# A hybrid encoder layer on one core: the first norm's scale moved behind the first eight tiles, and the final norm summed over five columns

## What is computed

```python
def rmsnorm(x, g):
    y = x * lax.rsqrt(jnp.mean(x * x, axis=-1, keepdims=True) + EPS)
    return y * g

h = rmsnorm(x, p['norm_mix'])
z = h @ w_in                       # 12 column groups; the first 1024 columns are q and k of the mLSTM
...                                # conv, mLSTM, forgetting attention, cross-attention, gates
mk, mv = split(rmsnorm(mem, g_mem) @ w_mem_kv, 2)
x = x + merged; x = x + peer(rmsnorm(x, p['norm_ffn']))
y = rmsnorm(x, norm_final)
```

## Time and profile before

| what | value |
|---|---|
| median of three runs | 2088.78 us |
| profiled execution | 2090.58 us |
| its span | 2088.9 us |
| TensorE busy | 2003.2 us (96%) |
| VectorE busy | 1430.3 us (68%) |
| ScalarE busy | 839.0 us (40%) |
| GpSimd busy | 818.8 us (39%) |
| chain of waits: TensorE / VectorE / DMA / ScalarE / GpSimd | 82 / 10 / 3 / 2 / 1% |
| first product of the first tile | 26.22 us |
| end of the last product of the experts' tiles | 2068.0 us |

### The profile page before, as it was taken

One profiled execution on the slowest core, in us unless ns is written; L12 is line 12 of the kernel. 1 busy time (PEld: TensorE's weight loads), 2 busy tenths in 40 slices (PEclk: granted clock), 3 DMA queues, 4 the chain that ended last, 5 costly groups with the idle time before them and its releaser, 6 DMA issues.

```text
span 2088.9 us, 34386 instructions
## 1 busy us (share of the span) xinstructions
PE 2003.2 (96%) x12642; PEld 1227.1 (59%) x12652; DVE 1430.3 (68%) x2691; ACT 839.0 (40%) x1244; POOL 818.8 (39%) x518
## 2 busy tenths in 40 slices
PE   5998998999999999999999999999999999999996
PEld 3745666667777787555555555555455555555553
DVE  5662555433336566989989989984787777777774
ACT  5334334344444433333345566563333333333331
POOL 5442111122234344465676667666343222222210
PEclk9999999999999999999999999999999999999998
DMA  5532112122334222456688999999999888888961
GB/s 200 138 128 94 41 41 85 68 80 72 137 126 146 102 72 75 148 202 232 213 330 314 353 360 358 354 351 397 382 369 372 332 328 329 329 332 334 346 232 46
DMA packets 180321, 467.12 MB, mean 224 GB/s; under 512 B 18600, under 2 KB 85168, under 8 KB 179448
## 3 DMA queue, kind: packets, MB, share of 16 engines
q1 hardware_dynamic: 102160, 248.28, 33.4%
q0 software_dynamic: 36864, 134.23, 17.5%
q10 hardware_dynamic: 41192, 83.22, 10.7%
HBM read 393.54 MB, written 72.14 MB: 223 GB/s over the span
## 4 chain that ended last, share of the span: by engine, by line
PE 82%; DVE 10%; DMA 3%; ACT 2%; POOL 1%; issue 1%; ACTq 0%; DVEq 0%
PE ps L1517 30%; PE ps L1904 27%; PE ps L1587 10%; PE ps L1533 3%; PE ps L1734 2%; DMA rows<-in_u_rows,rowi 1%; PE ps L1856 1%; PE ps L1857 1%; DVE rows L1363 1%; PE ps L1923 1%; PE ps L1699 1%; PE ps L1714 1%; POOL w_lo L485 1%; DVE hot L1425 1%; PE ps L1790 1%
## 5 line engine op out<-in xcount | busy, mean ns | idle before, releaser
L485 POOL TENSOR_TENSOR w_lo<-raw,w_hi 128x1024 bf16<-128x1024 f32 x229 | 508.5, 2223 | 760.9 <-ACT w_hi L570 759.8
L570 ACT ACTIVATE w_hi<-raw 128x1024 bf16<-128x1024 f32 x357 | 375.0, 1052 | 483.0 <-PE ps L1904 293.9
L1517 PE MATMUL ps<-act_hi,w_hi 128*128 128x448 bf16 (+1 forms) x1168 | 391.6, 346 | 9.8 <-DVE act_lo L973 8.6
L1517 PE MATMUL ps<-act_lo,w_hi 128*128 128x448 bf16 (+1 forms) x1168 | 391.4, 345 | 0.0
L1517 PE MATMUL ps<-act_hi,w_lo 128*128 128x448 bf16 (+1 forms) x1168 | 391.1, 345 | 0.0
L1904 PE MATMUL ps<-W_hi,w_hi 128*128 128x448 bf16 x992 | 350.3, 353 | 4.5 <-DVE W_lo L1465 4.5
L1904 PE MATMUL ps<-W_lo,w_hi 128*128 128x448 bf16 x992 | 350.3, 353 | 0.0
L1904 PE MATMUL ps<-W_hi,w_lo 128*128 128x448 bf16 x992 | 350.2, 353 | 0.0
L514 POOL DMA_INDIRECT rows<-in_v_units,rowi x128 | 151.4, 1183 | 412.2 <-DVE accS L1460 395.3
L1441 DVE TENSOR_TENSOR w_lo<-raw,w_hi 128x1024 bf16<-128x1024 f32 x128 | 156.7, 1224 | 115.4 <-ACT w_hi L570 110.5
L881 ACT ACTIVATE hb<-ps 128x448 f32<-128x448 f32 x128 | 69.6, 543 | 323.5 <-PE ps L1517 287.2
(11 more groups left out here) (355 smaller groups left out, 3197.3 us busy)
## 6 DMA issues: line engine op xcount, KB each, us to landing
raw<-in_u_units SPq DMA_DIRECT2D x128, 512.0 KB
raw<-in_v_units SPq DMA_DIRECT2D x128, 512.0 KB
raw<-in_units SPq DMA_DIRECT2D x101, 512.0 KB
hd<-hb ACTq DMA_DIRECT2D x128, 224.0 KB
gd<-gsb ACTq DMA_DIRECT2D x64, 448.0 KB
Gb<-gd SPq DMA_DIRECT2D x32, 896.0 KB
Hb<-hd SPq DMA_DIRECT2D x32, 896.0 KB
gz<-stage ACTq DMA_DIRECT2D x24, 288.0 KB, 2.1
```

What stands on the lines that cost most here:

```text
L485: pool.tensor_tensor(w_lo[:, k % RING, :], raw[:, k % RAW, :], w_hi[:, k % RING, :], ALU.subtract).then_inc(lo_ready, 1)
L570: act.activation(w_hi[:, k % RING, :], raw[:, k % RAW, :], ACT.Copy).then_inc(hi_ready, 1)
L1517: last = pe.matmul(ps[:, bank + half, 0:n], w[:, slot, col:col + P], x(k)[:, half * n:(half + 1) * n], start=(k == 0 and w is w_hi and x i ...
```

## The change

It has four parts.

1. **First eight tiles on x times the norm's weight.** ScalarE makes `raw_hi` = high half of x * par straight from x (an activation with the weight as scale), VectorE `raw_lo` by one operation. The eight tiles multiply with these, and `copy_tile` becomes a product: PSUM times `wk`, the row of 1/rms. The tiles turn over three pairs of banks (0 to 5), so tile k waits for the copy of tile k - 3. The squares, sums, root and rows of x are made while the tiles run: `x_sums`, `m_sums` and `x_rows` stand in tile 2, ahead of k = 1, 4 and 7. The rows of 1/rms are made in banks 6 and 7 and copied to `wk` by ScalarE. The normed activation itself (`mix_h`, `act_hi`, `act_lo`) is still made, between the copies; it is needed from the small tile on.
2. **VectorE makes the first four low halves.** GpSimd starts at unit 4, and only when VectorE has added both sets of squares.
3. **The memory's squares beside x's.** `mem_x` is issued by SyncE behind units 1 to 3, its squares follow unit 4 on ScalarE, its adds follow x's on VectorE. Unit 0 is issued by ScalarE between the two halves of x, `par` by SyncE ahead of everything; SyncE's first units wait for the second half of x, not the first. ScalarE loads the table of the square root at the very start.
4. **The final norm over five columns**, as in the norm before the experts. The adds of the squares no longer run one bank behind (`FIN_ADDS`); the eight products read 1/rms from PSUM.

The core of the diff:

```diff
@@ sync
-            sp.wait_ge(x_in[0], 16)
-            for n in range(RAW):
+            sp.dma_start(par[:, :], a["par"]).then_inc(par_in, 16)
+            sp.wait_ge(x_in[1], 16)
+            for n in range(1, RAW):
                 load(a["units"][n], n, True, 0)
+            sp.dma_start(mem_x[:, :, :], a["memT"]).then_inc(mem_in, 16)
@@ gpsimd
-            with pool.Fori(0, U_WQ // RING) as i:
+            pool.wait_ge(lo_ready, DVE_FIRST)
+            pool.wait_ge(n_add, 2 * (KT - 1))
+            for n in range(DVE_FIRST, RING):
+                low_half(n, n)
+            with pool.Fori(1, U_WQ // RING) as i:
@@ scalar
-            square(xT, mix_sq, lambda k: (x_in[k // (KT // 2)], 16))
+            act.activation(warm[:, 3:4], epsb[:, 0:1], ACT.Sqrt)
             act.wait_ge(par_in, 16)
-            for n in range(RAW):
+            for k in range(KT):
+                act.wait_ge(x_in[k // (KT // 2)], 16)
+                act.activation(raw_hi[:, k, :], xT[:, k, :], ACT.Copy, scale=par[:, C_MIX + k:C_MIX + k + 1]).then_inc(x_hi, 1)
+                if k == 1:
+                    high_unit(0)
+            for n in range(1, 4):
                 high_unit(n)
+                square(xT, mix_sq, None, range((0, 0, 3, 6)[n], (0, 3, 6, 8)[n]))
@@ vector
+            dve.wait_ge(n_rms, 1)
+            dve.reciprocal(rx[:, 1, :], rx[:, 0, :]).then_inc(n_inv, 1)
+            dve.wait_ge(r0_kept, 1)
...
-                dve.tensor_copy(proj[:, k, :].rearrange("p (a b) -> p a b", a=2),
-                                ps[:, 2 * (k % 2):2 * (k % 2) + 2, 0:HALF]).then_inc(t_evac, 1)
+                dve.tensor_tensor(proj[:, k, :].rearrange("p (a b) -> p a b", a=2),
+                                  ps[:, 2 * (k % 3):2 * (k % 3) + 2, 0:HALF],
+                                  wk[:, 1, :].rearrange("p (a b) -> p a b", a=2), ALU.mult).then_inc(t_evac, 1)
...
+            copy_tile(0)
+            copy_tile(1)
+            scaled(0, xT, C_MIX, ps[:, 6:8, :].rearrange("p a b -> p (a b)")[:, 0:T], mix_h, act_hi, act_lo,
+                   lambda k: copy_tile({3: 2, 7: 3}[k]) if k in (3, 7) else None)
+            copy_tile(4)
             norm(1, mem_x, C_MEM, wk[:, 0, 0:NMEM], mem_h, mem_hi, mem_lo)
-            for k in range(4, N_T):
+            for k in range(5, N_T):
                 copy_tile(k)
@@ tensor
             for k in range(N_T):
-                if k == 4:
-                    sums(1, mem_sq, [ps[:, 4, 0:NMEM]], NMEM)
                 pe.wait_ge(lo_ready, U_T + k + 1)
-                if k >= 2:
-                    pe.wait_ge(t_evac, k - 1)
-                tile((U_T + k) % RING, a_hi, a_lo, 2 * (k % 2), ready=None if k else 0).then_inc(unit_used, 1)
+                if k >= 3:
+                    pe.wait_ge(t_evac, k - 2)
+                tile((U_T + k) % RING, *xg0, 2 * (k % 3), ready=None if k else 0, split=x_lo,
+                     beside=((1, x_sums), (4, m_sums), (7, x_rows)) if k == 2 else ()).then_inc(unit_used, 1)
+            pe.wait_ge(n_lo, KT)
             pe.wait_ge(lo_ready, U_SMALL + 1)
+            pe.wait_ge(t_evac, N_T - 1)
             tile(U_SMALL % RING, a_hi, a_lo, 0).then_inc(unit_used, 1)
@@ vector and tensor, the end
+FIN_ADDS = {4: (1,), 5: (2, 3), 6: (4, 5), 7: (6, 7)}
+            pe.wait_ge(n_add, (KT - 1) * 4)
+            for t in range(NTT):
+                t0 = min(t * P, T - P)
+                last = pe.matmul(ps[:, t, 0:1], fin_sq[:, 0, t0:t0 + P], ones[:, 0:1], start=True, stop=True)
+            pe.wait_ge(n_inv, 4)
+            for t in range(4):
+                pe.matmul(row_[:, t * P:(t + 1) * P], tot[:, 1, t:t + 1].broadcast_to((P, P)), ident[:, :], start=True, stop=True)
```

More of the change, by code:

```diff
@@ L96 @@
 N_TK = 16
+DVE_FIRST = 4
 FIRST_W = {5: (0,), 6: (1,), 7: (2, 3)}
@@ L234, in program @@
         warm = sb("warm", [P, 4], F32)
+        rx = sb("rx", [P, 2, NTT], F32)
+        tot = sb("tot", [P, 2, NTT], F32)
         rT = sb("rT", [P, 2, NFT + 1], F32)
@@ L254, in program @@
         mem_lo = place("mem_lo", V0 + 4096, [P, KT, NMEM], BF16)
+        raw_hi = place("raw_hi", V0 + 8192, [P, KT, T], BF16)
+        raw_lo = place("raw_lo", V0 + 8192 + KT * T * 2, [P, KT, T], BF16)
         mkT = sb("mkT", [P, HC, NMEM], F32)
@@ L531, in _ @@
         def _(act):
[L532 to L535, removed]
+            act.dma_start(xT[:, 0:KT // 2, :], a["xT"][:, 0:KT // 2, :]).then_inc(x_in[0], 16)
+            act.dma_start(raw[:, 0, :], a["units"][0]).then_inc(raw_loaded[0], 16)
+            act.dma_start(xT[:, KT // 2:KT, :], a["xT"][:, KT // 2:KT, :]).then_inc(x_in[1], 16)
             def load_small():
@@ L956, in _ @@
             square(xT, fin_sq, lambda k: (acc_done, 5 if k < 4 else k + 3))
-            root(3, fin_r[:, :].rearrange("p (a b) -> p a b", a=2), ps[:, 2:4, 0:HALF])
+            root(3, tot[:, 0, :], ps[:, 0:NTT, 0:1].rearrange("p a b -> p (a b)"))
         @block.vector
@@ L966, in norm, with scaled @@
                 dve.wait_ge(n_inv, i + 1)
+                scaled(i, x, col, rs, h, hi, lo)
+            def scaled(i, x, col, rs, h, hi, lo, beside=lambda k: None):
                 for k in range(KT + 1):
+                    beside(k)
                     if k < KT:
@@ L1492, in _ @@
                                           xT[:, 4 * x:4 * x + 4, TD:T], ALU.add).then_inc(acc_done, 1)
-                if d >= 4:
-                    add_square(3, d - 3, fin_sq)
-            for k in range(KT - 3, KT - 1):
-                add_square(3, k, fin_sq)
-            norm(3, xT, C_FIN, fin_r[:, :], fin_y, None, None)
+                for k in FIN_ADDS.get(d, ()):
+                    add_square(3, k, fin_sq)
+            dve.wait_ge(n_rms, 4)
+            dve.reciprocal(tot[:, 1, :], tot[:, 0, :]).then_inc(n_inv, 1)
+            dve.wait_ge(r_spread, 1)
+            for k in range(KT):
+                dve.scalar_tensor_tensor(out=fin_y[:, k, :], in0=xT[:, k, :], scalar=par[:, C_FIN + k:C_FIN + k + 1],
+                                         in1=ps[:, 5:7, :].rearrange("p a b -> p (a b)")[:, 0:T],
+                                         op0=ALU.mult, op1=ALU.mult).then_inc(n_scaled, 1)
         @block.tensor
@@ L1507, in sums, with tile @@
                 last.then_inc(n_ssq, 1)
-            def tile(slot, rhs_hi, rhs_lo, bank, kts=KT, width=P, c0_=0, n=HALF, halves=2, ready=None, split=n_lo):
+            def tile(slot, rhs_hi, rhs_lo, bank, kts=KT, width=P, c0_=0, n=HALF, halves=2, ready=None, split=n_lo, beside=()):
                 for k in range(kts):
+                    for at, do in beside:
+                        if at == k:
+                            do()
                     if ready is not None:
```

75 lines of the change are left out of this document (50 added, 25 removed).

## The result

The changed kernel takes **2074.4 us** (median of 5 runs, 2072.76 to 2078.8) against 2088.78 (2085.83 to 2089.61, 5 runs): ratio 0.9936, 95% interval 0.9923 to 0.9948, so 14.4 us by the medians, 11 to 16 by the interval. The forecast was 2067.4 with a range to 2074.0: the sign is right, the gain is two thirds of the 21.4 forecast. The profiled execution took 2072.76 us.

What follows compares the result with a forecast made beforehand. TensorE (96% busy) was taken as the bound, with waits of size only at start and end. Gains of 17.4 and 4.0 sum to 21.4 us, moving the median from 2088.78 to 2067.4; range 2062 to 2074.

Steps and rivals of the forecast that it cites:

- The start: From launch to the first tiles: first product at 10.1 us, 16.1 us earlier, with full clock by 14.
- the wait before tile 3: At the fourth of the first eight tiles: TensorE arrives at 33.4 us and waits 0.9 us for VectorE's scaled tile 0.
- The small tile's wait: Before the small tile, from 63.8: TensorE waits 2.3 us for copy 6, plus half of 1.6 us for a lower clock.
- Rival 1: No wait before the small tile, memory's first tile at 69.7: gain 20.4 plus 4.0, time 2064.4 us; chance 20%.
- The end: Final norm, last add to first output product at 2075.6 us: 4.0 us gained, bounds 3.1 and 5.7.
- whatever TensorE gains by the memory's first tile, it keeps: After the memory's first tile: TensorE bounds everything until the end, so the 17.4 us gained by then stay.
- rival 3: Weight units arrive late behind the tiles, through GpSimd's pace or a held ScalarE: 8 to 17 us lost, 2076 to 2085; 4%.
- edits at nothing: Wider bank rotation, `mem_x` on SyncE's queue and GpSimd's later start: counted as costing no time.
- my 17.4: Forecast gain in us by the memory's first tile, which starts at 72.7 against 90.11.
- Rivals 2: At the start, unit 0 or `par` lands late, or the clock is low before the small tile: 2071.9 us; 20%.
- 4 (the lower clock stays): In the first tiles the lower clock level persists, making the kernel slower: 2120 us if all nine stayed low; chance 2%.
- 5: The first eight tiles wait for the row of 1/rms after all: about 2085 us; chance 1%.

Runs made afterwards that it cites:

- packed kernel: Changed kernel with both conv outputs first copied together by VectorE and written in 96-byte runs: 2061.7 us, ratio 0.9879; again 2062.2 us, 0.9887.
- second profile: The changed kernel unaltered, measured again on one chip beside other versions: 2073.09 us, ratio 0.9933 to the kernel before.
- units first: Changed kernel with the high halves of units 12 to 15 made ahead of the nine small loads on ScalarE: 2075.19 us, ratio 0.9955.
- small loads late: Changed kernel with the nine small loads moved behind the memory values on ScalarE: 2069.22 us, ratio 0.9926.

## Why the prediction was right or wrong

**The start** was right step by step: first product 10.1 forecast, 10.20 measured; full clock by 14, measured at 14.43; the wait before tile 3 0.9 at 33.4, measured 0.78 at 32.85. `par` landed 4.2 us after issue, so the first half of x ended the wait, as assumed. `m_sums` took 0.43 us at full clock, not 1.0.

**The small tile's wait** was sized too large: 0.73 us instead of 2.3 and 0.8 for the clock. VectorE's memory norm met GpSimd in three operations, as forecast, but ended at 62.4 instead of 64.4, and copy 6 at 63.8 instead of 66.0. Rival 1, with its 69.7 for the memory's first tile, is what happened (69.80). The condition I had set for it, that GpSimd's halves fall beside other work, was only partly met: VectorE came to the memory's norm at 48.79 instead of 50.4, which is most of the difference. The 1.6 us for a lower clock behind this wait stand in the forecast without a row for their size; the granted clock from 64 to 68 us was 1.00. VectorE's new copies took 0.74 to 0.75 us, as assumed.

**The end** was right: 4.0 forecast, 4.0 measured in kernels that differ only in it, 4.7 between the first two profiles. Within it the column sums took 1.26 us where 2.1 were assumed, the rows 2.68 for 2.4.

**The step that failed** is the sentence on which the sum rests: "whatever TensorE gains by the memory's first tile, it keeps". It kept 5.3 of 20.3 us in the profiled pair. The packed kernel, whose front differs in its packets, still has 19.3 of them at the first product behind the `mv` copies (139.53 us before, 134.22 after, 120.25 packed), so the collision costs **14.0 us** there (13.3 against the changed kernel's second profile). The mechanism is rival 3, *units arrive late behind the tiles*, which I gave 4% and priced at 8 to 17 us, but with the wrong culprit: I looked at GpSimd's pace and at ScalarE's time, not at what else stands in the DMA queues when the eighth tile ends 20 us sooner. The part of the text on edits at nothing names the units 12 to 15 that GpSimd still has to make, and costs them at nothing; that they are made so late, because ScalarE comes to unit 12 only at 65.77, is what puts the load of unit 16 behind the conv outputs, and these the text does not mention. (Asking 4 us sooner, as with the units first or the small loads late, was not enough to be clear of them.) They were to be seen in the profile before, 12 KB with 8.6 and 11.0 us to landing.

Rival 3 put the time at 2076 to 2085 (its 8 to 17 us on top of the forecast would be 2075.4 to 2084.4), because it took the loss from my 17.4. With the true terms, 20.3 + 4.0 - 14.0 = 10.3 us, the time would be 2078.5; measured are 13.4 us by the first ratio (11 to 16) and 14.0 by the second (10 to 18). That the time came out only 0.4 us above the stated range is luck: the collision alone, on top of the forecast, makes it 2081.4, and 2.9 us more at the start and the rest of 3 to 4 us, neither of them forecast, made up for about half of it.

That rest is of the size by which executions of one kernel differ. From the first product behind the `mv` copies to the one behind the pause at 348 us, where the change touches nothing, the kernel before took 210.9 us at a mean granted clock of 0.94, and 207.8 at 0.95 with its outputs packed; the changed kernel took 203.5 at 0.97 in its first profile, 206.8 at 0.95 in its second, and 210.8 at 0.94 with the old final norm. One place shows how. A pause of 0.83 us, in the same work, ends at 234.39 before, at 226.62 in the changed kernel's first profile and at 224.38 in its second; here are the same stretches about it, by the view of windows, in this order:

```profile
230.00:245.00 15.00, 14.17 (x56) 8.15 (x55) 6.94 (x13) 4.01 (x10) 2.12 (x1) 0.66 0.18 66
```

```profile
222.00:237.00 15.00, 14.17 (x83) 9.39 (x81) 8.42 (x16) 5.25 (x13) 2.12 (x1) 1.00 0.19 69
```

```profile
220.00:235.00 15.00, 14.17 (x54) 8.12 (x53) 6.94 (x13) 4.02 (x10) 2.12 (x1) 0.65 0.19 65
```

The lower level followed before and in one of two executions of the changed kernel, so it does not come with the change here. Whether such stretches are rarer on average after it stays open: in that part of the program the twelve profiles with the new start took 201.9 to 210.8 us, the two with the old one 207.8 and 210.9. Rivals 2 (first data late), 4 (the lower clock stays) and 5 did not happen.

## What to carry to other kernels

When a change lets one engine run ahead, list every transfer issued in the stretch that it now reaches early, by packets as well as by bytes, and ask which load is issued behind it and who waits for that load: here 24 KB of outputs in 2048 pieces cost 14 of the 20 us gained, and two small VectorE copies that pack them won these back. If a pause seems to come from the order alone, move the waiting work once before believing it, since a late load shows up wherever its first user stands.

## What was not expected of the hardware

The cost of packets: 1024 packets of 12 bytes to memory, issued 3 us ahead, lengthened a 512 KB load on another engine's queue from 4.4 us to 11.0, and the next 1024 to 15.65 or 16.4. If they are spread over the 16 DMA engines, which no view here shows, that is 64 each at 72 to 103 ns, an estimate from these loads. The same bytes in runs of 96 left the unit loads at 4.4 to 4.7 us. The Trainium skill ("DMA: Bandwidth & Descriptors", "Issuing engines are not separate DMA queues") says that transfers of all issuing engines run on the same 16 DMA engines and interleave; by that rule, the trace agrees, since the load was on SyncE's queue and the outputs on ScalarE's. The same page ("Why small descriptors are slow (HBM only)") gives about three cycles of overhead for each packet and, for each DMA operation, 32 bytes of metadata; no run here separates these.

The issue itself can be held: the second conv output took 8.37 us to issue in the kernel with the units first, against 0.90 in the changed one, and ScalarE stood still with it. What it waited for no view shows.
